# Late division in dilated attention, and head-by-head steps with late gates in stick-breaking attention

## The reference

```python
# first block: dilated attention, 8 heads of 64, softmax over biased scores
s = q @ k.T + bias; s = where(mask, s, NEG)
m = s.max(-1); p = exp(s - m); den = p.sum(-1); o = (p @ v) / den
h = h + concat(gla, dilated) @ w_out            # "wo0", "wo1"

# second block: stick-breaking attention, 8 heads of 64
z = q @ k.T * scale                             # strictly causal
sp = where(causal, softplus(z), 0)
rest = cumsum(sp, reverse) - sp
w = exp(log_sigmoid(z) - rest); o = w @ v
# gates of its other mixer, from columns of the same product x_n @ w_in
q_hg = silu(q_in)                               # "hq"
f = lb + (1 - lb) * sigmoid(f_in); key = 1 - f; log_f = log(f)    # "hf"
val = i_in; gate = silu(g_in)                   # "vH", "hg"
```

## Time and profile before

| what | value |
|---|---|
| median of 3 runs | 1363.39 us (1362.97 to 1363.85) |
| profiled execution, its own time | 1364.07 us |
| its span in the trace | 1362.7 us |
| PE busy | 1348.6 us (99%) |
| DVE, ACT, POOL busy | 873.2, 819.9, 334.6 us |
| granted clock of TensorE | 1.00 |

### The profile page before, as it was taken

How to read it: one execution, slowest core, us unless ns; L and a number is a source line. 1 busy time by engine, 2 the same in 40 slices (tenths; PEclk the granted TensorE clock), 3 DMA queues, 4 the chain that set the end, 5 groups by cost and what they waited for, 6 DMA issues and landing times.

```text
span 1362.7 us, 19539 instructions
## 1 busy us (share of the span) xinstructions
PE 1348.6 (99%) x7510; PEld 1135.7 (83%) x7510; DVE 873.2 (64%) x1548; ACT 819.9 (60%) x1235; POOL 334.6 (25%) x306
## 2 busy tenths in 40 slices
PE   9999999999999999999999999999999999999999
PEld 6977956789899898887777788888888898889889
DVE  6055466577576682357787779975437785568557
ACT  6575566753544545666577767775666645754553
POOL 0211101235343251111211121211113252315214
DMA  7976643925436137876654685668888536824733
GB/s 251 238 165 144 148 117 78 231 32 196 99 98 179 33 125 191 193 169 144 149 129 111 137 217 125 137 145 182 201 214 203 110 118 194 184 47 164 188 51 109
DMA packets 57969, 202.45 MB, mean 149 GB/s; under 512 B 6450, under 2 KB 7019, under 8 KB 57748
## 3 DMA queue, kind: packets, MB, share of 16 engines
q0 software_dynamic: 25632, 93.09, 36.4%
q1 hardware_dynamic: 31380, 106.24, 23.7%
q10 hardware_dynamic: 864, 1.87, 0.4%
HBM read 199.05 MB, written 2.12 MB: 148 GB/s over the span
## 4 chain that ended last, share of the span: by engine, by line
PE 77%; DVE 11%; ACT 8%; DMA 3%; issue 2%; SPq 0%; POOL 0%; DVEq 0%; ACTq 0%
PE bank L660 18%; PE bank L667 18%; PE bank L664 18%; PE bank L698 17%; DVE eb L1730 2%; PE bank L813 1%; ACT WL L1038 1%; ACT eb L1198 1%; ACT WH L1030 1%; ACT zs L1152 1%; PE bank L885 1%; DVE eb L1725 1%; DMA WL<-in_w_in 1%; DMA WL<-in_w_gu 1%; DMA RAW<-in_w_in 1%
## 5 line engine op out<-in xcount | busy, mean ns | idle before, releaser
L660 PE MATMUL bank<-NH,WH 128*128 128x512 f32 x1152 | 459.8, 400 | 0.3 <-ACT NH L1207 0.3
L664 PE MATMUL bank<-NL,WH 128*128 128x512 f32 x1152 | 448.1, 390 | 0.6 <-DVE NL L1470 0.5
L667 PE MATMUL bank<-NH,WL 128*128 128x512 f32 x1152 | 448.1, 390 | 0.6 <-DVE WL L1465 0.4
L660 PEld LDWEIGHTS bank<-NH,WH 128*128 128x128 f32 x1152 | 216.5, 188 | 60.2 <-issue 17.8
L667 PEld LDWEIGHTS bank<-NH,WL 128*128 128x128 f32 x1152 | 216.2, 188 | 47.5 <-DVE WL L1465 0.8
L664 PEld LDWEIGHTS bank<-NL,WH 128*128 128x128 f32 x1152 | 216.8, 188 | 44.7 <-DVE NL L1470 1.6
L1030 ACT ACTIVATE WH<-RAW 128x1024 fp32r<-128x1024 f32 (+3 forms) x148 | 152.1, 1032 | 74.4 <-PE bank L667 39.0
L698 PE MATMUL bank<-AH,WH 128*128 128x256 f32 x644 | 182.5, 283 | 0.3 <-DVE AL L2115 0.3
L698 PE MATMUL bank<-AL,WH 128*128 128x256 f32 x644 | 182.2, 283 | 0.0
L698 PE MATMUL bank<-AH,WL 128*128 128x256 f32 x644 | 182.2, 283 | 0.0
L1038 ACT ACTIVATE WL<-WH 128x1024 fp32r<-128x1024 f32 (+1 forms) x146 | 153.3, 1052 | 12.2 <-DMA WH<-in_w_in 9.9
(11 more groups left out here) (375 smaller groups left out, 2115.3 us busy)
## 6 DMA issues: line engine op xcount, KB each, us to landing
WL<-in_w_in POOLq DMA_DIRECT2D x58, 512.0 KB, 7.2
RAW<-in_w_gu SPq DMA_DIRECT2D x44, 512.0 KB, 5.1
WL<-in_w_gu POOLq DMA_DIRECT2D x34, 512.0 KB, 8.0
RAW<-in_w_ff SPq DMA_DIRECT2D x32, 512.0 KB, 4.6
WH<-in_w_in POOLq DMA_DIRECT2D x32, 512.0 KB, 7.1
RAW<-in_w_in SPq DMA_DIRECT2D x28, 512.0 KB, 6.4
quarters<-in_w_ff SPq DMA_DIRECT2D x24, 512.0 KB, 4.7
WL<-in_w_ff POOLq DMA_DIRECT2D x17, 512.0 KB, 6.5
```

Source lines behind the costliest of these rows:

```text
L660: e.matmul(o, a[0], a[1], start=(k == 0), stop=False)
L664: e.matmul(o, b[0], b[1], start=False, stop=False)
L667: mm = e.matmul(o, c[0], c[1], start=False, stop=(k == t.kt - 1))
```

## The change

1. **Dilated attention.** A function `early(s)` is true for step 0 and for the row 2 steps. For all other steps ("late rows") the division moves on DVE from ahead of the next step's reading of the scores to behind it. PE's transposes get a due time R1/4 later than the value products (`apart` is now true), with the scores at R1/2 as they were, and ACT's copies and late exponentials get due times later by R1/4.
2. **Stick-breaking attention.** On DVE, masking and absolute value now alternate head by head, and so do scan and subtraction.
3. **Gates.** The last gate steps of hq, hg (on DVE), hf (on DVE and ACT's logarithm) get later due times.

```diff
+        def early(s):
+            return s == 0 or ORDER[s][1] == MIDDLE
...
-                attention("dil", T_A1, R1, R1 / 2, False, qD, kD, vD, zs, pT, lambda hp: freed(plan.stage["qD"][hp]),
+                attention("dil", T_A1, R1, R1 / 4, True, qD, kD, vD, zs, pT, lambda hp: freed(plan.stage["qD"][hp]),
...
-                        yield T_A1 + R1 * s + 0.15
+                        yield T_A1 + R1 * s + R1 / 4 + 0.15
                         n = WIDTH[s - 2]
...
-                    if 1 <= s <= NA and ORDER[s - 1][1] != MIDDLE:
-
-                        yield T_A1 + R1 * s + 0.17
+                    if 1 <= s <= NA and not early(s - 1):
+
+                        yield T_A1 + R1 * s + R1 / 4 + 0.17
                         exponentials(s - 1)
-                    if s < NA and ORDER[s][1] == MIDDLE:
+                    if s < NA and early(s):
                         yield T_A1 + R1 * s + R1 * 2 / 3 + 0.02
                         exponentials(s)
...
-                    yield calm(t, 9.2)
+                    yield calm(t, 11.5)
                     act.wait_ge(("hf_f", t.i))
...
-                    yield calm(t, 11.0 if st == "hg" else 9.0)
+                    yield calm(t, 9.0 if st == "gG" else 11.3)
                     dve.wait_ge(("sigmoid", (st, t.i)), ("evac_v", t.g))
...
+            def divide(s):
+                dve.wait_ge(("dil_e", s))
+                e.reciprocal(step_stats(s, 3), step_stats(s, 2)).then_inc(*dve.sig("dil_r", s))
+                dve.wait_ge(("dil_r", s))
+                for p in range(2):
+                    for i, at_ in ORDER[s][1]:
+                        x, z = row_stat(s, i, p), zs[2 * (s % 2) + p][:, at_:at_ + (i + 1) * P]
+                        mul = e.tensor_scalar(z, z, x[:, 3:4], None, ALU.mult)
+                    mul.then_inc(*dve.sig("dil_p", s, p))
...
-                    if 1 <= s <= NA:
-                        dve.wait_ge(("dil_e", s - 1))
...
+                    if 1 <= s <= NA and early(s - 1):
+                        divide(s - 1)
                     if s < NA:
                         yield T_A1 + R1 * s + R1 * 2 / 3
...
+                    if 1 <= s <= NA and not early(s - 1):
+                        yield T_A1 + R1 * s + R1 * 2 / 3 + 0.01
+                        divide(s - 1)
...
                             scan.then_inc(*dve.sig("stick_sum", s - 1, p))
-                        for p in range(2):
                             dve.wait_ge(("stick_sum", s - 1, p))
                             e.tensor_tensor(z[p], z[p], ee[p], ALU.subtract).then_inc(*dve.sig("stick_log", s - 1, p))
...
                             low_.then_inc(*dve.sig("stick_b", s, p))
-                        for p in range(2):
                             dve.wait_ge(("stick_b", s, p))
...
-                    yield calm(t, 9.0)
+                    yield calm(t, 11.3)
                     dve.wait_ge(("sigmoid", ("hf", t.i)), ("lb", 6))
```

More of the change, by code:

```diff
@@ L1685, in dilated @@
                         heads_out("dil", s - 3, lambda hp: mixed[:, 4 + hp, :], [("band_stored",)])
-                    if 1 <= s <= NA:
-                        dve.wait_ge(("dil_e", s - 1))
-                        e.reciprocal(step_stats(s - 1, 3), step_stats(s - 1, 2)).then_inc(*dve.sig("dil_r", s - 1))
-                        dve.wait_ge(("dil_r", s - 1))
-                        for p in range(2):
[L1691 to L1694, removed]
+                    if 1 <= s <= NA and early(s - 1):
+                        divide(s - 1)
                     if s < NA:
```

## The result

| | median | runs |
|---|---|---|
| before | 1363.82 us | 1362.63 to 1364.39 (11) |
| after | 1366.83 us | 1364.51 to 1368.75 (11) |

The ratio is 1.0021 with a 95% interval of 1.0011 to 1.0030: the change makes the kernel 3.0 us slower by the medians, 2.9 by the ratio. I had forecast 1363.0 and most likely no difference. The time lies inside the range given, but the forecast of no difference was wrong.

What follows compares the result with a forecast made beforehand. PE, busy 99% of the span, was taken to bound the kernel, with late DVE/ACT chains making it stand. Profiled 1364.07 - 4.7 (stick) + 4.2 (dilated) = 1363.6, as a median 1363.0 us; range 1358.8 to 1367.2, no-difference band 1360.7 to 1366.1.

Steps and rivals of the forecast that it cites:

- The clock falls: Rival, dilated stage: three PE stands bring half clock, 2 us each, 1369 us; chance 0.03.
- PE standing 2.1 us at steps 5 and 8: Dilated stage: the late division, behind NH, NL and the reading, makes PE stand 2.1 us at each step.
- The dilated waits: Dilated stage: waits added by late divisions, less waits removed, cost +4.2 us.
- the 2.9 to 3.0 removed: Dilated stage: PE's waits for the reading, two copies and step 11's old division wait go, 2.9 to 3.0 us.
- My 202.4: Dilated stage, step 5: the division's first head is ready at 202.4, where before it was 200.2.
- at step 6 none (0.87): Dilated stage, step 6: PE waits 0.87 us for the division, behind step 5's late transposes and L1038.
- The stick stage: Stick stage: a shorter DVE and ACT loop removes PE's waits for vH and wT, -4.7 us.
- a rule of pairs at no cost: Stick stage: if dependent DVE pairs cost nothing, a gated step gains 1.0 us, not 0.5; end changes by some tenths.
- The wait for NH doesn't bind: Faster rival, dilated stage: level or up to 1 us gained, about 1358.3 us; chance 0.20.
- The stick stage gives nothing: Slower rival, stick stage: the loop's lead doesn't reach PE, 1367.1 us; chance 0.19.
- Both stages come to nothing: Rival, both stages: PE's slack eats either effect, 1363.4 us; counted with the forecast's band.
- The slower rival: Stick stage: its gain doesn't come to PE, 1367.1 us; chance given as 0.19, then 0.17.

Runs made afterwards that it cites:

- e4_filler: The change plus 16, 16 and 10 transposes of a constant on PE ahead of the division waits of steps 5, 8 and 11; 1364.27 us.
- e3_low_half_behind: The change with the low half NL of finished heads moved on DVE from ahead of the next reading to behind the late division; 1360.08 us.
- e1: The kernel before with only the stick-breaking head-by-head order and the late gates, dilated stage as before; 1360.24 us, ratio 0.9968.
- e6: The kernel before with only the late gates (hq, hg, hf and its logarithm); 1359.70 us, ratio 0.9964.
- e10: The change without head-by-head order, with NL behind the late divisions and PE's and ACT's dilated order as before the change; 1358.05 us.
- e7: The change plus 16 transposes of a constant on PE ahead of the wait of step 5's transposes alone; 1365.89 us.

## Why the prediction was wrong

**The sum and its failing step.** I wrote: "The clock falls", with "No stretch at a lower clock exists in the windows to price it" and a chance of 0.03. That is the step that failed. I had forecast the cause itself, PE standing 2.1 us at steps 5 and 8 where its longest wait had been 1.3, and treated the sum as if PE went on at its full clock behind it. The runs show that it doesn't: it is 2.4 us of the stage's 7.3, by the run with fillers, in an execution with two falls. Without it the change measures as its filler version does, 1364.3, inside the band of no difference. Once the forecast contained a stand longer than any in the trace of before, the trace's 1.00 was no evidence for what comes behind it, and the clock belonged into the main case or into one with a chance like the other rivals'. The price given there was three times 2 us; there were at most two falls in the traces, and half the clock for 3.2 to 3.4 us costs 1.6 to 1.7 each, less what other waits absorb.

**The dilated waits were right, one size off.** Forecast +4.2; with the clock at full speed the stage measured +4.9 (e4_filler); the term is 0.7 too small. A part of that is in the sum: its terms add up to 7.3, and less the 2.9 to 3.0 removed that is 4.3 to 4.4, not 4.2. The rest, about 0.5, I have not split further. DVE stood 3.57 us for NH, with ACT's L1149 as the releaser, exactly as drawn:

```profile
200.45 0.69 DVE L1673 TENSOR_TENSOR NL<-mixed,NH 128x512 fp32r<-128x512 f32 x1 [3.57 <-ACT NH L1149]
201.05 0.28 DVE L1713 CUSTOM_DVE_ANT_0 zs<-bank,toep 128x128 f32<-128x128 f32 x1
...
202.35 0.17 DVE L1717 TENSOR_SCALAR small<-small 128x4 f32<-128x4 f32 x1
202.43 0.16 DVE L1685 RECIPROCAL small<-small 128x2 f32<-128x2 f32 x1
202.62 0.88 DVE L1690 TENSOR_SCALAR zs<-zs,small 128x512 f32<-128x512 f32 x2
```

From here the steps are 0.60 (NL), 1.30 (reading), 0.08, 0.19 and 0.55 until PE goes on at 203.17. My 202.4, plus the 0.46 by which the whole trace is late, is 202.9. The stands were 2.01 + 0.17 = 2.2 at steps 5 and 8 (2.1 forecast), 1.39 + 0.17 = 1.6 at step 11 (1.9), and at step 6 none (0.87), the last because PE ran slow; at full clock it is 0.77 + 0.17.

**The stick stage was right as a sum.** -4.7 forecast, -4.65 measured. Softplus begins in the step of 512 at 754.03, 1.2 us behind the last absolute value, where the earlier trace rows has 3.2:

```profile
752.12 0.69 DVE L1760 SCALAR_TENSOR_TENSOR eb<-zb 128x512 f32<-128x512 f32 x1
754.03 1.29 DVE L1735 SCALAR_TENSOR_TENSOR eb<-zb,eb 128x512 f32<-128x512 f32 x2 [1.22 <-ACT eb L1206]
```

Its inner terms held in part. I had capped the gain by PE's stalls: gates alone give 5.1 on PE, where the stalls were 4.7. I wrote that a rule of pairs at no cost "would change the end by some tenths only": next to late gates, undoing the pairs gave 0.5 on PE within the stage, and 1.7 by ratios whose intervals overlap. Without late gates the pairs cost 5.6 by the ratio, and PE's waits for ACT grow with it. The Trainium skill's sentence that the next Vector instruction starts when the pipe is empty ("VectorE: DVE Perf Modes", "The DRAIN you can't avoid"), which I read as pairs at no cost, doesn't fit: 0.11 to 0.13 each in the trace, and 2.5 and 3.1 us in two runs that do nothing else. The same section adds that an instruction which isn't held back starts earlier, and the trace agrees with that: 0.60 from one to the next where the rows themselves are 0.69 long. A dependent instruction loses this head start: in the pairs above it starts 0.03 to 0.04 us behind the end of the first.

**The rivals.** "The wait for NH doesn't bind": it binds; where it is taken away (e3_low_half_behind) the time is 1360.1, near that rival's 1358.3. "The stick stage gives nothing": refuted by e1. "Both stages come to nothing": no, each moved by over 4 us, in opposite directions.

**The chances.** The slower rival has 0.19 in its own line and 0.17 in the sum of the chances; the result hangs on neither.

**Open.** What decides whether a stand of 2 us brings the clock down. Of the 5.1 us that the gates alone give on PE within the stage, 4.7 are the stalls of the earlier trace rows with their tails; the last 0.4 comes in steps of under 0.2 us and is not traced to a cause. After the stage PE gains another 0.7 us between 812 and 823 in the traces of e6 and e10, and not in those with the pairs (e7 loses 1.0 there). The traces are single executions, so that I can't say whether this last part is real; it could explain why the ratios put e10 further ahead of e8 than 0.5.

## What to carry to other kernels

Where an edit reorders an engine, list everything that comes to stand between the old place and the new one, and ask of each what it waits for: a copy that waits for another engine, in three steps, cost more here than the whole edit could give, and moving that copy brought it back. If the forecast itself makes the matrix engine stand longer than it ever stood in the trace, price what its clock does behind that; work of no use in the gap can be cheaper than the gap (1364.3 against 1366.8 us here). And alternate two independent chains on VectorE stage by stage (both masks, then both absolute values) instead of chain by chain (the other order cost 5.6 us here by itself), unless the next engine truly waits for the first.

## What was not expected of the hardware

In the profiled execution the granted clock went to 0.50 (1.2 GHz) at the end of stands of PE of 2.0 us, for 3.2 to 3.4 us, in two places of a stage that runs at 1.00 otherwise; by the mean clocks of the launches it did so in some of them and not in others. It stayed at 1.00 behind stands of 1.0 and 1.4 us. In the run with the dilated part alone the first transposes behind the second stand ran at full clock, and the fall came 1.3 us after the stand's end at 218.75 (0.52 in the microsecond from 220 is 0.96 of it at half clock):

```profile
219.00:220.00 1.00, 1.00 (x10) 1.00 0.00 0
220.00:221.00 1.00, 1.00 (x5) 0.52 0.00 0
221.00:222.00 1.00, 1.00 (x4) 0.50 0.00 0
```

The rule of the Trainium skill ("TensorE: Matmul & The Clock Gate", "Part 1: The HAM clock gate") that an idle engine loses its clock agrees with that in kind. A dependent successor on DVE cost 0.11 to 0.13 us over an independent one: 0.11 behind a mask, 0.13 behind a scan and behind the multiplication of the earlier trace rows.
